# Output projection of the gated MLP: chunks 2 and 3 of each half as one pair of seven products

## The reference, cut to what matters

```python
y = u * mixed * jax.nn.silu(zg)      # 256 x 4096
h = h + y @ w_out                    # w_out: 4096 x 2048
hn = rms_norm(h, norm_g[1])          # input of the attention layer
proj = hn @ w_in                     # its first columns are q
```

## Time and profile before

| | |
|---|---|
| median of 3 runs | 2556.36 us (2556.3 to 2557.05) |
| profiled execution | 2556.51 us |
| its span, first to last instruction | 2554.7 us |
| TensorE, weight loads | 2548.8 us, 2113.5 us |
| VectorE, ScalarE | 1794.1 us, 1304.9 us |
| granted clock of TensorE, mean | 1.000 |
| DMA | 527.43 MB, 206 GB/s |

### The profile page before, as it was taken

The page is one execution under the profiler, slowest core; times in us unless marked ns, Lnnn a source line. Parts: engine busy times, 40 slices in busy tenths (PEclk is TensorE's granted clock), DMA queues, the critical chain, the costliest instruction groups (busy, mean ns, idle before and its releaser), DMA issues.

```text
span 2554.7 us, 29496 instructions
## 1 busy us (share of the span) xinstructions
PE 2548.8 (100%) x11413; PEld 2113.5 (83%) x11413; DVE 1794.1 (70%) x2098; ACT 1304.9 (51%) x1563; POOL 34.8 (1%) x56
## 2 busy tenths in 40 slices
PE   9999999999999999999999999999999999999999
PEld 8888888888888888888888888888888888888887
DVE  6866565566666666776876877678678768778686
ACT  6654443444545555455444544445465455455463
POOL 1000000000000000000000000000020000000000
PEclk9999999999999999999999999999999999999999
DMA  8667766676777777777565787666757677667674
GB/s 286 206 202 201 207 203 195 191 212 199 217 214 202 213 197 205 218 223 226 165 188 175 207 226 207 196 206 198 243 173 225 197 212 214 215 195 225 205 231 141
DMA packets 534796, 527.43 MB, mean 206 GB/s; under 512 B 294896, under 2 KB 297824, under 8 KB 534656
## 3 DMA queue, kind: packets, MB, share of 16 engines
q1 hardware_dynamic: 531856, 518.09, 68.1%
q0 software_dynamic: 2384, 6.93, 1.1%
q10 hardware_dynamic: 416, 0.52, 0.1%
HBM read 488.24 MB, written 2.10 MB: 192 GB/s over the span
## 4 chain that ended last, share of the span: by engine, by line
PE 100%; ACT 0%; DVE 0%; issue 0%
PE bank L2364 30%; PE bank L2365 30%; PE bank L2366 30%; PE bank L2431 2%; PE bank L2432 2%; PE bank L2433 2%; PE bank L2550 1%; PE bank L2539 1%; PE bank L2529 1%; PE bank L2463 0%; PE bank L2472 0%; PE bank L2485 0%; PE bank L2478 0%; PE bank L2610 0%; PE bank L2597 0%; PE bank L2630 0%
## 5 line engine op out<-in xcount | busy, mean ns | idle before, releaser
L1284 DVE TENSOR_TENSOR t_wl<-t_stage,t_wh 128x1024 fp32r<-128x1024 f32 x840 | 1016.9, 1220 | 567.6 <-ACT t_wh L718 562.0
L718 ACT ACTIVATE t_wh<-t_stage 128x1024 fp32r<-128x1024 f32 x841 | 881.3, 1057 | 784.3 <-PE bank L2366 737.5
L2364 PE MATMUL bank<-t_wl,t_xth 128*128 128x512 f32 x2368 | 928.5, 392 | 0.5 <-DVE t_xtl L1326 0.5
L2366 PE MATMUL bank<-t_wh,t_xtl 128*128 128x512 f32 x2368 | 921.7, 389 | 0.0
L2365 PE MATMUL bank<-t_wh,t_xth 128*128 128x512 f32 x2368 | 921.5, 389 | 0.0
L2366 PEld LDWEIGHTS bank<-t_wh,t_xtl 128*128 128x128 f32 x2368 | 444.4, 188 | 93.0
L2364 PEld LDWEIGHTS bank<-t_wl,t_xth 128*128 128x128 f32 x2368 | 444.6, 188 | 92.3 <-DVE t_xtl L1326 0.9
L2365 PEld LDWEIGHTS bank<-t_wh,t_xth 128*128 128x128 f32 x2368 | 444.6, 188 | 91.4 <-issue 0.2
L2364 PE MATMUL bank<-t_wl,t_yth 128*128 128x512 f32 x914 | 355.6, 389 | 0.0
L2365 PE MATMUL bank<-t_wh,t_yth 128*128 128x512 f32 x914 | 355.1, 389 | 0.0
L2366 PE MATMUL bank<-t_wh,t_ytl 128*128 128x512 f32 x914 | 355.1, 389 | 0.0
(11 more groups left out here) (430 smaller groups left out, 1608.6 us busy)
## 6 DMA issues: line engine op xcount, KB each, us to landing
t_stage<-in_a_w_in_dram SPq DMA_DIRECT2D x182, 512.0 KB, 4.4
t_stage<-in_w_in_dram SPq DMA_DIRECT2D x168, 512.0 KB, 4.4
t_stage<-in_b_w_in_dram SPq DMA_DIRECT2D x128, 512.0 KB, 4.4
t_stage<-in_w_up_dram SPq DMA_DIRECT2D x92, 512.0 KB, 4.5
t_stage<-in_w_down_dram SPq DMA_DIRECT2D x90, 512.0 KB, 5.4
t_stage<-in_a_w_out_dram SPq DMA_DIRECT2D x64, 512.0 KB, 4.4
t_ubuf<-in_w_down_dram SPq DMA_DIRECT2D x38, 512.0 KB, 5.2
t_ubuf<-in_w_up_dram SPq DMA_DIRECT2D x36, 512.0 KB, 4.5
```

Of the source, the lines that this page charges most:

```text
L718: e.activation(wh[:, j % N_SPLIT], stage[s], ACT.Copy).then_inc(*hi(j))
L1284: e.tensor_tensor(low, src, high.bitcast(F32), ALU.subtract).then_inc(*lo(j))
L2364: e.matmul(o, h, w_l, start=start, stop=False)
L2366: return e.matmul(o, l, w_h, start=False, stop=stop)
```

## The change

Two pairs are added to the list, (("a_out", h, 2), ("a_out", h, 3)) for h = 0 and 1. Their token sums are made of y's first four k-tiles of the half, in a region (`vreg`) that the half's values of v have left; two tiles of that region serve as further staging buffers from the second chunk of the half to the start of the pair. The products are collected in `buf[0]` and `buf[1]` and added to `hres` ahead of the pair's own sums ("early"). In half 1, the steps that prepare chunks 2 and 3 for "q" are put behind the pair's end.

```diff
 def halved_pairs():
 
     return ([(("v", c), ("v", c + 1)) for c in (4, 6)] +
+            [(("a_out", h, 2), ("a_out", h, 3)) for h in range(2)] +
...
+    vtile = (vreg[:, 1024:2048].rearrange("p (a b) -> p a b", a=2), vreg[:, 5120:6144].rearrange("p (a b) -> p a b", a=2))
+    stage = [stage_[:, i] for i in range(N_STAGE)] + [ubuf[:, 0], ubuf[:, 1], spare[:, 0], spare[:, 1], pool4[:, 3], rowb,
+                                                      vtile[0], vtile[1]]
...
+    for h in range(2):
+        opens["a_out", h, 1] = [(s, 2, lambda h=h: prod.at("mix", 4 * h + 3, 1)) for s in (11, 12)]
+        closes["a_out", h, 2] = (11, 12)
...
+        if name[0] == "a_out":
+            return ("y", name[1]), mth[:, 0:4, :], mtl[:, 0:4, :], vreg[:, 4096:5120]
...
-        if kind in ("gm", "up"):
+        if kind in ("gm", "up", "a_out"):
             return [buf[n // 2][:, n % 2, :] for n in range(4)]
...
@@ scalar @@
+            if c == 3:
+                slot(end("a_out", 0, 0) + 3)
+                sum_high("y", 0)
+                apart(first_of["a_out", 0, 2], turned.at("y", 3))
         for c in range(4):
             slot(end("a_out", 1, c) + 2)
             e.wait_ge(*vec.at("h", 1, c))
             for i in range(2):
                 squares(hres[:, i, cols(c)], ssq[:, i, c:c + 1], "h", c, i)
-            slot(end("a_out", 1, c) + (5 if c == 3 else 4))
+            if c == 0:
+                slot(end("a_out", 1, 0) + 3)
+                sum_high("y", 1)
+            if c == 1:
+                apart(first_of["a_out", 1, 2], turned.at("y", 7))
+            slot(end("a_out", 1, c | 1) + (2, 4, 2, 5)[c] if c > 1 else end("a_out", 1, c) + 4)
             gained_highs(c, g_b, "xb", c)
...
@@ vector @@
-            for c in range(4):
+            def out_sum(c):
                 slot(end("a_out", h, c))
                 e.wait_ge(*used.at(end("a_out", h, c) - 1))
                 for i in range(2):
                     hr = hres[:, i, cols(c)]
                     e.tensor_tensor(hr, hr, accs("a_out", h, c)[i], ALU.add).then_inc(
                         *vec("h", h, c) if i else vec())
...
+            def out_turn(c):
+                slot(end("a_out", 1, c) + 1)
+                e.wait_ge(*vec.at("h", 1, c))
+                turn_chunk(lambda i: hres[:, i, cols(c)], flat[zt_buf[c]], "xb", c)
+
+            m = first_of["a_out", h, 2]
+            out_sum(0)
+            if h:
+                out_turn(0)
+            slot(end("a_out", h, 0) + 2)
+            split_sums(yth, ytl, vreg[:, 0:1024], vreg[:, 4096:5120], "y", h)
+            if h:
+                slot(end("a_out", h, 0) + 4)
+                gained_lows(0, g_b, "xb", 0)
+            slot(end("a_out", h, 0) + 5)
+            sum_low("y", h)
+            out_sum(1)
+            if h:
+                out_turn(1)
+            slot(end("a_out", h, 1) + 2)
+            together(m, turned.at("y", 4 * h + 3))
+            if h:
+                slot(end("a_out", h, 1) + 4)
+                gained_lows(1, g_b, "xb", 1)
+            slot(end("a_out", h, 1) + 7)
+            e.wait_ge(*vec.at("w", "pair", m))
+            for c in (2, 3):
+                d = hres[:, :, cols(c)]
+                e.tensor_tensor(d, d, buf[c - 2], ALU.add).then_inc(*vec("early", m, c))
+                e.wait_ge(*vec.at("early", m, c))
+            out_sum(2)
+            if h:
+                out_turn(2)
+            out_sum(3)
+            if h:
+                out_turn(3)
+                slot(end("a_out", 1, 3) + 2)
+                gained_lows(2, g_b, "xb", 2)
+                e.wait_ge(*square.at("h", 3, 1))
+                norm_scale(sB, hB, ssq, 4, D, "sB")
+                e.wait_ge(*vec.at("sB"))
+                e.tensor_scalar(sBq, sB, float(128.0 ** -0.5), None, ALU.mult).then_inc(*vec("sBq"))
+                slot(end("a_out", 1, 3) + 5)
+                gained_lows(3, g_b, "xb", 3)
```

More of the change, by code:

```diff
@@ L173, in _program @@
     hold, _ = sb("hold", [16, S], offset=s_at + 4096 + 2112)
-    stage = [stage_[:, i] for i in range(N_STAGE)] + [ubuf[:, 0], ubuf[:, 1], spare[:, 0], spare[:, 1], pool4[:, 3], rowb]
     ident, _ = sb("ident", [128, 128])
```

## The result

| | before | changed |
|---|---|---|
| median of 20 runs | 2556.59 us (2556.23 to 2557.70) | 2560.26 us (2559.28 to 2561.73) |
| ratio | 1 | 1.0015, 95% interval 1.0009 to 1.0021 |
| profiled execution (span) | 2556.51 (2554.7) | 2561.39 (2559.7) |

The change makes the kernel slower by 3.7 us, 0.15%: less than the 0.2% that the prediction took as the least that can be told apart, yet with twenty runs each it is clear of noise. The forecast was +1.9 us, 2558.2, its range 2553.4 to 2560.8; the time lies in the range, on rival B's figure of 2560.1. One of the eleven executions of the reordered version further down took 5246 us and is left out where its runs are grouped.

The account below looks back on a forecast made before the run. TensorE is hardly ever without work, so the kernel is the sum of its matmuls. Matmuls -2.72, waits +0.82 (half 0) and +3.76 (half 1) make +1.9 us: 2558.2 against the median, range 2553.4 to 2560.8.

Parts of the forecast that it names:

- rival B: The clock falls in TensorE's pause of half 1: nothing to 1.9 us more, up to 2560.1 us; chance 0.25.
- What bounds the kernel: Whole kernel: TensorE busy 2548.8 of 2554.7 us; only fewer matmuls win time, any new wait is lost in full.
- The matmuls: Both halves' new pairs: twelve matmuls fewer at 0.227 us each, -2.72 us.
- The wait at P5: Each pair's second pass waits for the token sums' low part on VectorE: 0.82 us in half 0, 3.76 in half 1.
- The beginning of "q": After half 1: chunk 3's low parts start 14.1 us after its end, 1.7 us left, cost nothing.
- rival C: After half 1, "q" waits for chunk 3's low parts, delayed by about one more transfer: 2562.0 us; chance 0.08.
- VectorE's extra work: Both pairs' added splits, sums, differences and adds: 17.8 us per pair, 36 us in all, hidden as a total.
- The transfers: The pairs' weight loads, 16 of 512 KB per pair with two more buffers: cost nothing, hidden behind seven buffers' lead.
- The clock: After the pause of half 1: the sum held no term for a clock fall.
- only a little of it lies beyond those 3 us: Argument against a clock fall in half 1: the 3.8 us pause barely exceeds the 3 us within which the tail's clock fell.
- Rival A: No wait appears at the pairs' second pass, only the removed matmuls count: 2553.6 us; chance 0.17.

Follow-up runs that it names:

- reordered version: Changed kernel with, in half 1, the token sums' low part put ahead of chunk 0's low parts, both still behind the same splits: 2559.67 us.
- the early version: Changed kernel with, in both halves, the token sums' low part moved right behind the sums and the splits up to F+6: 2553.85 us, repeated 2553.66.
- half 0 alone: Changed kernel with the pair kept only in half 0, half 1 as before the change: 2556.39 us, 0.9999 of the kernel before.

## Why the prediction was right, and where not

**What bounds the kernel: right.** The pauses and the matmuls taken away show in the time one for one, to some 0.3 us (the table above, the early version, half 0 alone).

**The matmuls: right.** -2.72 was worked out; the version without waits stands 2.7 and 2.9 us below the kernel before. The row's pace of 0.227 is seen again in the trace after. The gain of 2.59 us by the figure of the Trainium skill (TensorE: Matmul & The Clock Gate, "Wait — 56ns, not 53.3ns?") can't be told from it by these medians; the pace in the trace can.

**The wait at P5: right in place, cause and size.** In half 0 0.82 was worked out and 0.91 measured. From the subtraction's end (400.74) to the first matmul (400.88) there are 0.14 us that the prediction took as nothing. In half 1 3.76 was worked out and 3.79 measured, and the rows come in the order written down. The early version confirms the cause: with the wait both the pause and the fall of the clock are gone.

**The beginning of "q": right.** Chunk 3's low parts were to start 14.1 us after the end of the half; they start at 737.51, and the half ends at 723.06 (TensorE's 24 matmuls after chunk 2's end at 717.62): 14.5. TensorE doesn't wait; rival C did not come. VectorE's extra work was put at 36 us and is 33.5.

**The transfers: nothing, as costed,** but only because of the two buffers: without them the kernel takes 3.4 us more.

**The clock: the term that was mis-sized.** The sum put it at nothing, as the likeliest case; rival B had it with 0.25 and up to 1.9 us. Measured, it is 1.8 us at the median, half of the change's +3.7, and shows in 19 of the 20 runs; the lowest, 2559.28, is 0.8 above the time with the clock kept. The time lies in the range because B had been let into it. The step that failed is the argument "only a little of it lies beyond those 3 us". I read one fall in the tail's rows, 2.2 us after the last matmul (2551.0 to 2553.2), as one that needs some 2 to 3 us of idleness to come. A pause of 2.58 us brings it in six of eleven runs, and it comes 2.3 to 5.2 us after the pause begins, before or after the restart. The bound, half of a low stretch as long as the pause, gave 1.9 by luck: in the profiled execution the clock was low for 6.8 us, 1.6 of them before the restart, and after a pause of 6.4 us the extra is 2.4 and not 3.2. With B as the likeliest case the forecast would have been 2560.1.

The Trainium skill (TensorE: Matmul & The Clock Gate, "The HAM clock gate") says that idleness returns the array to half rate and that work releases it. The tail showed the fall alone; the windows after show both, 0.50 from near 670 and full again near 677.

Rival A, no wait, was wrong for the change and is what the early version is.

## What to carry to other kernels

Where one engine has all the time, a step that saves work on it is worth its saving only if each value it reads is ready: list for each new read what stands ahead of its producer on its own queue, and put the producer ahead of preparations for later groups. Count the buffers as part of the change: without the two added ones the early version takes 3.4 us more. In these runs a pause of TensorE of 1.3 us cost about its length, one of 2.6 us in half of the runs 1.7 us more, and those of 3.8 to 6.4 us nearly always 1.8 to 2.4 us more; between 1.3 and 2.6 us nothing was measured. When a change of this kind comes out even or slower, move the late producer before giving the change up: here one moved call was worth 6.4 us.

## What was not expected of the hardware

The clock can fall after TensorE has resumed: with a pause of 2.6 us it went from 1.00 to 0.50 about 1 us after the restart and was back some 3.4 us later (the starts lie 0.427 us apart from 670.3 to 673.3). At the same pause length the times of eleven runs form two groups, six with a granted clock of 0.999 (the profiled one, which shows the fall, is among them) and five with 1.000. They differ by 1.7 us; the slow steps of the trace lose 1.6.

The length of the low stretch doesn't follow the length of the pause. It was 3.4 us in the three profiled executions with the fall after the restart and 6.8 us in the three with the fall inside the pause, for pauses from 2.6 to 6.4 us. What decides between the two is not shown.
